# Gate and up products of 32 experts with the weights standing and 112 tokens moving

## The reference, cut to what matters

```python
logits = (xt @ w_router + b_router)              # 512 x 32
top_vals, top_idx = lax.top_k(logits, 4)
def expert_block(args):                          # xb: the tokens of expert e
    gate = xb @ w_gate[e] + b_gate[e]            # 1024 x 1024
    up = xb @ w_up[e] + b_up[e]                  # 1024 x 1024
    gate = jnp.minimum(gate, 7.0)
    up = jnp.clip(up, -7.0, 7.0)
    glu = gate * jax.nn.sigmoid(1.702 * gate)
    return (glu * (up + 1.0)) @ w_down[e] + b_down[e]
```

## Time and profile before

| | |
|---|---|
| median of 3 runs | 1819.93 us (1819.75 to 1820.05) |
| span of the profiled execution (first to last instruction) | 1819.7 us |
| TensorE matmuls busy | 1772.5 us, 97% of the span, 8267 instructions |
| TensorE weight loads busy (overlap the matmuls) | 1425.3 us, 78% |
| VectorE busy | 1425.9 us, 78% |
| ScalarE busy | 1174.5 us, 65% |
| GpSimd busy | 202.7 us, 11% |
| memory read and written | 481.95 MB and 21.36 MB |
| mean granted clock of TensorE | 0.989 of full |

### The profile page before, as it was taken

How to read it: one execution, slowest core, us unless ns; L and a number is a source line. 1 busy time by engine, 2 the same in 40 slices (tenths; PEclk the granted TensorE clock), 3 DMA queues, 4 the chain that set the end, 5 groups by cost and what they waited for, 6 DMA issues and landing times.

```text
span 1819.7 us, 20820 instructions
## 1 busy us (share of the span) xinstructions
PE 1772.5 (97%) x8267; PEld 1425.3 (78%) x8267; DVE 1425.9 (78%) x1236; ACT 1174.5 (65%) x883; POOL 202.7 (11%) x139
## 2 busy tenths in 40 slices
PE   7999889999999999999999999999998999999998
PEld 5777768888888888888888888888884777778887
DVE  4577689999999999999999999999895524775343
ACT  4354558777877777777777777777773346665232
POOL 1412011112111111211111121111001000000000
PEclk9999989999999999999999999999998999999999
DMA  7312369999999999999999999999996322122221
GB/s 271 125 47 81 131 239 373 372 363 365 385 365 363 379 375 367 368 372 372 360 373 374 362 368 379 370 365 369 380 359 238 129 80 70 46 76 93 93 81 47
DMA packets 96291, 487.96 MB, mean 268 GB/s; under 512 B 14376, under 2 KB 16080, under 8 KB 46272
## 3 DMA queue, kind: packets, MB, share of 16 engines
q1 hardware_dynamic: 81696, 462.64, 67.5%
q0 software_dynamic: 10288, 18.19, 2.7%
q10 hardware_dynamic: 4208, 5.77, 0.9%
HBM read 481.95 MB, written 21.36 MB: 277 GB/s over the span
## 4 chain that ended last, share of the span: by engine, by line
PE 94%; DVE 3%; ACT 2%; issue 1%; DMA 1%; ACTq 0%; SPq 0%; DVEq 0%; POOLq 0%
PE PS L455 86%; PE PS L692 3%; PE PS L872 1%; PE PS L884 1%; DVE WL L1251 0%; PE PS L567 0%; PE PS L865 0%; DMA ring<-in_w_in_dram 0%; PE PS L487 0%; DVE X L1596 0%; DVE Pp L1686 0%; DMA xg<-h2d,tok 0%; ACT Pp L1183 0%; ACT L1181 0%; ACT PH L1186 0%
## 5 line engine op out<-in xcount | busy, mean ns | idle before, releaser
L1251 DVE TENSOR_TENSOR WL<-ring,WH 128x2048 fp32r<-128x2048 f32 x428 | 967.3, 2286 | 217.5 <-ACT WH L937 211.5
L937 ACT ACTIVATE WH<-ring 128x2048 fp32r<-128x2048 f32 x428 | 818.6, 1915 | 350.7 <-PE PS L455 338.9
L455 PE MATMUL PS<-WH,xh 128*128 128x512 f32 x1024 | 326.6, 400 | 2.2 <-ACT xh L1078 2.2
L455 PE MATMUL PS<-WL,xh 128*128 128x512 f32 x1024 | 318.4, 392 | 0.0
L455 PE MATMUL PS<-WH,xl 128*128 128x512 f32 x1024 | 275.6, 391 | 0.0
L455 PEld LDWEIGHTS PS<-WH,xl 128*128 128x128 f32 x1024 | 192.8, 188 | 41.8
L455 PEld LDWEIGHTS PS<-WL,xh 128*128 128x128 f32 x1024 | 192.8, 188 | 41.7
L455 PEld LDWEIGHTS PS<-WH,xh 128*128 128x128 f32 x1024 | 185.8, 189 | 44.1 <-issue 7.2
L1850 POOL DMA_INDIRECT yd<-ys,dst x32 | 80.7, 2522 | 960.9 <-ACT ys L1095 960.9
L455 PE MATMUL PS<-WH,hh 128*128 128x512 f32 x512 | 160.5, 394 | 1.1 <-ACT hh L1078 1.1
L455 PE MATMUL PS<-WL,hh 128*128 128x512 f32 x512 | 158.4, 390 | 0.0
(11 more groups left out here) (350 smaller groups left out, 2099.7 us busy)
## 6 DMA issues: line engine op xcount, KB each, us to landing
ring<-in_w_gate_dram SPq DMA_DIRECT2D x128, 1024.0 KB, 7.5
ring<-in_w_up_dram SPq DMA_DIRECT2D x128, 1024.0 KB, 7.2
ring<-in_w_down_dram SPq DMA_DIRECT2D x128, 1024.0 KB, 8.4
ring<-in_w_in_dram SPq DMA_DIRECT2D x32, 1024.0 KB, 5.4
ring<-in_w_out_dram SPq DMA_DIRECT2D x8, 1024.0 KB, 5.0
yk<-yd SPq DMA_DIRECT2D x4, 1024.0 KB, 8.4
X<-in_x_dram SPq DMA_DIRECT2D x4, 512.0 KB, 9.5
h2d<-HV ACTq DMA_DIRECT2D x4, 512.0 KB, 2.8
```

What stands on the lines that cost most here:

```text
L455: return P.matmul(ps, a, b, start=start, stop=stop)
L937: A.activation(WH[buf[n]], ring[spot[n]], ACT.Copy).then_inc(s_hi, 1)
L1251: V.tensor_tensor(WL[buf[n]], ring[spot[n]], WH[buf[n]].bitcast(F32), SUB).then_inc(s_lo, 1)
```

## The change

Gate and up swap operands. In `features_by_slots` a 128 x 128 block of the weights stands, and the 112 places of the expert move past it; a piece has 2 x 8 such blocks, each with three matmuls (low weights x high tokens, high x high, high x low), so 48 matmuls of 112 columns in place of 12 of 512. The outputs lie by feature, 4 blocks of 128 features in a bank. So the inner rows come out as the down product wants them: the second transposes go, and `hh` and `hl` are made from `eu` itself. The bias matmuls become 16 of 112 columns. The down product keeps its form, with 112 standing columns in place of 128; its weights are loaded in another row order (4 KB runs in place of 8 KB). Gate and up of an expert now wait for both parts of the turned rows at their start, not for the low part after the first 8 matmuls. All tiles by place hold 112 places (`NB`); an expert with more tokens would go to the slow loop.

```diff
-    xh = reg("xh", [128, 8, 128], F32R, 8)
-    xl = reg("xl", [128, 8, 128], F32R, 12)
+    xhl = reg("xhl", [128, 8, 2, NB], F32R, 8)
...
+    def features_by_slots(n, kc, b0):
+
+        wh, wl = by_rows(WH[buf[n]]), by_rows(WL[buf[n]])
+        P.wait_ge(s_lo, n + 1)
+        for k in range(2):
+            kk = 2 * kc + k
+            for c in range(8):
+                o = PS[:, b0 + c // 4, 128 * (c % 4):128 * (c % 4) + NB]
+                f = slice(128 * c, 128 * c + 128)
+                P.matmul(o, wl[:, k, f], xhl[:, kk, 0], start=(kk == 0 and c % 4 == 0 and b0 == 0), stop=False, skip_group_check=True)
+                P.matmul(o, wh[:, k, f], xhl[:, kk, 0], start=False, stop=False, skip_group_check=True)
+                last = P.matmul(o, wh[:, k, f], xhl[:, kk, 1], start=False, stop=(kk == 7 and b0 == 2), skip_group_check=True)
+        return last
...
     def tensor_gate_up(e):
-        P.wait_ge(s_th, t_rows[e] + 1)
+        P.wait_ge(s_th, e + 1)
+        P.wait_ge(s_tl, e + 1)
...
-            last = rows_by_columns(n_g[e] + p, kc, 2 * which, xh, xl, 0 if p else t_rows[e] + 1)
+            last = features_by_slots(n_g[e] + p, kc, 2 * which)
...
-                for n in range(4):
-                    rows = slice(32 * n, 32 * n + 24)
-                    last = mm(PS[:, n, :], sel8[rows, e % 8:e % 8 + 1].broadcast_to([24, 128]), b3[rows, e // 8], n >= 2, n < 2)
+                for c in range(4):
+                    for n in range(4):
+                        rows, f = slice(32 * n, 32 * n + 24), slice(128 * c, 128 * c + 128)
+                        last = P.matmul(PS[:, n, 128 * c:128 * c + NB], b3[rows, e // 8, f], sel8[rows, e % 8:e % 8 + 1].broadcast_to([24, NB]),
+                                        start=(n >= 2 and c == 0), stop=(n < 2), skip_group_check=True)
...
@@ def tensor_experts():
             if e:
                 tensor_down(e - 1)
-            if 0 < e < E:
-                tensor_turn_mid(e)
...
+    def scalar_hidden(e):
+        A.wait_ge(s_eh, e + 1)
+        if e:
+            A.wait_ge(s_mm, done[n_d[e - 1] + 4])
+        A.activation(hh, eu, ACT.Copy).then_inc(s_hh, 1)
...
+    def vector_hidden(e):
+        V.wait_ge(s_hh, e + 1)
+        V.tensor_tensor(hl, eu, hh.bitcast(F32), SUB).then_inc(s_hl, 1)
```

More of the change, by code:

```diff
@@ L107, in program @@
     fl = place("fl", [128, 16], F32)
-    ovm = place("ovm", [128, E, 3], F32)
+    ovm = place("ovm", [128, E, 4], F32)
     nov = place("nov", [128, 2], F32)
@@ L192, in program @@
     xg = [reg(f"xg{i}", [128, D], F32, 4 * i) for i in range(2)]
-    xh = reg("xh", [128, 8, 128], F32R, 8)
-    xl = reg("xl", [128, 8, 128], F32R, 12)
[L195 to L198, removed]
+    xhl = reg("xhl", [128, 8, 2, NB], F32R, 8)
+    hh = reg("hh", [128, 8, NB], F32R, 16)
+    hl = reg("hl", [128, 8, NB], F32R, 20)
+    eg = reg("eg", [128, 8, NB], F32, 24)
+    eu = reg("eu", [128, 8, NB], F32, 28)
     ys = [reg(f"ys{i}", [128, 2, 512], F32, 32 + 4 * i) for i in range(2)]
-    oh = [reg(f"oh{i}", [128, 4, 128], F16, 40 + i) for i in range(3)]
+    oh = [reg(f"oh{i}", [128, 4, NB], F16, 40 + i) for i in range(3)]
     iv = reg("iv", [128, 4], F32, 43)
@@ L284, in whole_rows, with row_blocks @@
         return len(pieces) - 4
+    def row_blocks(w):
+        for kc in range(4):
+            pieces.append(w[256 * kc:256 * kc + 256].rearrange("(k p) f -> p k f", k=2))
+            done.append(done[-1] + 1)
+        return len(pieces) - 4
     W1, W2 = w_in[0], w_in_2[0]
@@ L411, in load @@
         o = ring[spot[n]]
-        S.dma_start(o.rearrange("p a f -> p (a f)") if first <= n < second else o, pieces[n]).then_inc(s_ring[spot[n]], 16)
+        if first <= n < second:
+            o = o.rearrange("p a f -> p (a f)") if len(pieces[n].shape) == 2 else by_rows(o)
+        S.dma_start(o, pieces[n]).then_inc(s_ring[spot[n]], 16)
     def sync_first():
@@ L685, in tensor_index @@
         for j in range(4):
-            last = mm(PS[:, bank, 0:1], oh[q % NI][:, j], DV16[:, j, q:q + 1], j == 0, j == 3)
+            last = mm(PS[0:NB, bank, 0:1], oh[q % NI][:, j], DV16[:, j, q:q + 1], j == 0, j == 3)
         last.then_inc(s_im, 1)
[L689 to L693, removed]
     def tensor_turn_rows(e):
@@ L703, in tensor_turn_rows, with slots_by_columns @@
             P.wait_ge(s_spk, 1)
[L704 to L711, removed]
+        pairs_ = xg[e % 2][0:NB].rearrange("t (c p k) -> t c k p", p=128, k=2)
+        for k in range(8):
+            last = P.transpose(PS[:, 6 + k // 4, 128 * (k % 4):128 * (k % 4) + NB], pairs_[:, k // 2, k % 2], C[0:NB, IDENT:IDENT + NB])
+        last.then_inc(s_tt, 1)
+    def features_by_slots(n, kc, b0):
[10 more added lines that the diff above has]
+        return last
+    def slots_by_columns(n, kc, waited):
         wh, wl = by_rows(WH[buf[n]]), by_rows(WL[buf[n]])
@@ L718, in rows_by_columns @@
                 for hf in range(2):
-                    mm(PS[:, b0 + hf, :], hi[:, kk], w[:, k, 512 * hf:512 * hf + 512], kk == 0 and w is wh and b0 != 2, False)
-        if turned:
-            P.wait_ge(s_tl, turned)
+                    mm(PS[0:NB, 4 + hf, :], hh[:, kk], w[:, k, 512 * hf:512 * hf + 512], kk == 0 and w is wh, False)
+        if kc == 0:
+            P.wait_ge(s_hl, waited)
         for k in range(2):
@@ L724, in rows_by_columns @@
             for hf in range(2):
[L725 removed]
+                last = mm(PS[0:NB, 4 + hf, :], hl[:, kk], wh[:, k, 512 * hf:512 * hf + 512], False, kk == 7)
         return last
     def tensor_gate_up(e):
[L729 removed]
+        P.wait_ge(s_th, e + 1)
+        P.wait_ge(s_tl, e + 1)
         for p in range(8):
@@ L754, in tensor_gate_up @@
             if p == 4:
-                P.wait_ge(s_tl, t_mid[e - 1] + 1 if e else 1)
+                P.wait_ge(s_tl, e + 1)
                 if e + NI < E:
@@ L790, in tensor_down_bias @@
         P.wait_ge(s_bd, 16)
-        P.wait_ge((s_eg, s_eu, s_ys, s_tl)[j], E if j < 3 else 2 * E)
+        P.wait_ge((s_eg, s_eu, s_ys, s_tl)[j], E)
         for hf in range(2):
@@ L1492, in vector_further_count @@
         V.wait_ge(s_cnt, 1)
-        for j in range(3):
-            last = V.tensor_scalar(ovm[:, :, j], cnt, 128.0 * (j + 1), None, ALU.is_gt)
+        for j in range(4):
+            last = V.tensor_scalar(ovm[:, :, j], cnt, float(NB + 128 * j), None, ALU.is_gt)
         last.then_inc(dv.sem, dv.one())
```

106 lines of the change are left out of this document (53 added, 53 removed).

## The result

The changed kernel takes 2557.8 us (median of 4 runs, 2557.1 to 2559.4) where the kernel before takes 1820.0 in the same runs: 1.405 times the time, 95% interval 1.4035 to 1.4069. The forecast was 2553 in a range of 2435 to 2780, with 0.97 for slower. The profiled execution has a span of 2555.8 us, 736.1 more than before, and a mean clock of 0.959.

A forecast was written before the change was run, and what follows sets the result against it. TensorE was taken to bound the kernel at 35.50 us an expert. 1819.7 + 650 for 32 dearer experts + 81 for half clock + 2.5 for waits gave 2553 us, range 2435 to 2780.

The forecast's parts named there:

- Gate and up: Gate and up products of each expert: 384 matmuls at 0.112 us, 43.01 us after for 21.84 before, +21.17 us.
- the router's row: Profile row of the router's 32 matmuls of 32 columns, without a gap, loads every 0.112 us; taken as the matmul price.
- The other price: Gate and up at the skill's 81 ns for load and matmul: 31.1 us an expert, kernel near 2150 us; not followed.
- Down: Down product of each expert: keeps 48 matmuls of 512 columns at 10.94 us.
- transposes: Transposes in each expert: the second set goes, -0.95 us; the first keeps its 8 instructions and 0.95 us.
- The clock: Gate and up of experts 0 and 1: 768 matmuls at half clock until expert 0's down product, +81 us.
- The least sure step: Gate and up after experts 0 and 1: the clock, once restored, holds through 43 us of narrow matmuls.
- this rival: Gate and up of every expert: the narrow run loses the clock, 42 us more for 30 experts, 3810 us; chance 0.14.
- The rival that it comes back in the first gates: Experts 0 and 1: the array is never idle, so the clock returns and 81 us don't come due; 2472 us, chance 0.08.
- Shared loads: Gate and up: two matmuls naming the same WH block share one load, 256 loads, about 2070 us; chance 0.06.
- Faster: Gate and up with loads fully hidden: 0.053 us a matmul, memory traffic then holds an expert at 34.4, 1785 us; chance 0.02.
- The waits: Gates of experts 0 and 1 wait for the low part of the turned rows, 1.22 us showing; +2.5 us in all.

## Why the prediction was right, step by step

- **Gate and up**, 384 x 0.112 = 43.01 from the router's row: measured 43.00. With the small matmuls I had 43.93, measured 43.47: the sixteen bias matmuls and the four of the index take 0.47 us, where I had set aside 0.92 for all that is not one of the 384. Taking the price from a dense run of narrow float32 matmuls, and not from a width, was the step that carried 32 x (43.47 - 22.66) = 666 of the 738 us; the runs of half a block and of 64 columns show that it is the load.
- **The other price**, the 81 ns that the Trainium skill gives for 128 columns in "TensorE: Matmul & The Clock Gate", section "Back-to-back issue gap", does not hold for these operands: 112 ns with 112 and with 128 columns. The measurement decides. (The prediction's "near 2150" has the clock's term shrink along with the price; with the rest of the sum as it stands it would be 2172.)
- **Down** 10.94, measured 11.10; **transposes** 0.95, measured 1.02. An expert 55.8, measured 55.59; 32 of them +643 for +650.
- **The clock**, +81: measured 2 x 40.4 = 81, from 0.50 in both experts' gates and ups as forecast. The price at half clock was 0.213 and not 0.218, which makes 2 x 38.8; the small matmuls, slower there and more of them than in mid-kernel (bias, index, in expert 1 the turn of the routing weights), bring it to about the same sum. The clock came back at 416, forecast 410.
- **The least sure step**, that it then holds: it held. That was a choice between two rows, and the run with 64 columns shows how much hung on it: 3680 us. The 0.14 on this rival was not too much. So this step came out right as a guess, not as something worked out.
- **The rival that it comes back in the first gates**, 2472: it fell. 83.9 us without a gap did not restore it, nor did the next 83.8. The rule behind that rival, in the Trainium skill's "TensorE: Matmul & The Clock Gate", section "Why this matters for your kernels", asks for no idle gaps. Here a gap did lose the clock (the pause between experts 0 and 1), but the absence of gaps neither won it back nor, with 64 columns, kept it. The reason that I gave against the rival was weaker than it read: ahead of the router's run TensorE had been idle for 1.0 of the 4 us from 213 to 217, so the earlier trace rows do not tell whether that run or those gaps lost the clock. The run with 64 columns shows a gapless narrow run doing it.
- **Shared loads**, 2070: the changed kernel did not do it; made by hand, it gave 2078.5, in which the stretches outside the experts are again dearer than before.
- **Faster**: the break-even was 0.0593 us a matmul. The half block ran at 0.059 and came out at 1826.9, 0.35% above the kernel before. From the first gather to the last down it takes 1144.5 us, 4 less than the kernel before, in spite of the clock's loss at the start; the rest, 10 us more, lies outside the experts.
- **The waits** for the low part at experts 0 and 1: forecast 2.5. The chain shows 1.22 us twice (this is the second; the row that is called issue is TensorE's wait):

```profile
324.85 1.55 PE PS L708 x8
326.43 0.93 ACT xhl L1097
327.36 1.22 issue
328.57 0.43 PE PS L720
```

- **Costed at nothing and not so**: all stretches outside the experts. They grew by 9.7 us, and the places of tiles are why. The sum was for the span of the profiled execution, 2553 for 2555.8, and its closeness is partly luck: the experts came out 7 us cheaper than forecast, and what lies outside them 9.7 dearer.

## What to carry to other kernels

Before swapping the standing with the moving operand, count loads times standing columns: in a dense run each 128-column fp32r load costs 0.112 us, and a matmul of fewer moving columns than that covers only waits for it; here 384 loads replaced 96 matmuls whose loads were hidden. Ask of every run of narrow matmuls behind an idle stretch which clock it starts with: here it stayed at half clock, or at full, according to how it began, and a handful of wide matmuls in the pauses was worth 76 us. Don't take that for a rule without looking, since with half the load the same matmuls won the clock back by themselves, and with 64 moving columns they lost it. And when a stretch that no edit touched grows by 2%, look at what the edit did to the places of tiles.

## What the runs showed of the hardware that I had not expected

- TensorE at half clock stayed there through 168 us of narrow matmuls in which its row had no gap but the one turn of rows; 512-column ones directly behind brought it back in 2.2 us. With half the standing columns the same 112-column matmuls brought it back themselves, in 4.2 and 6.1 us. The narrow matmuls with full loads, begun at 1.00, kept it for 43.8 us, and, with a down product between each two experts, for 30 experts on end. With 64 moving columns for 112 they lost it in each expert.
- The clock was lost at a pause of 3.2 us with 1.02 us of work in it, and kept where wide matmuls filled the pause.
- Half the standing columns is half the load: 0.059 us for 0.112. At half clock it was 0.213 with 128 standing columns and 0.107 with 64.
- 512-column fp32r matmuls took 0.227 or 0.232 us depending on whether the tiles behind the tables lay 103168 or 103296 bytes from the ring; 25 us in the kernel before. With weight buffers that moved along with the rows it stayed 0.227. A shift of all by 32 bytes changed nothing. A standing tile of 112 columns with its slices 448 bytes apart gave 0.230.
